# State mixer of a two-block network kernel: chunk-state pairs reordered so that half of them swap array columns, and lag kernels built two chunks at a time

## The chip, the cores and the metric

The kernel runs on one core of a Trainium2 chip. The metric is the device time of one execution in microseconds (us). Before the change the median of three executions is 1320.17 us (1318.69 to 1329.96).

## What is computed

The reference is a chain of layers over 512 tokens of width 1024: a block with a pooling mixer, a gated delta rule and a squared-ReLU feed-forward part, a sparse-attention layer, and then the layer that the change touches, a diagonal state-space mixer (`_s5_mixer`). Everything is float32. That mixer, cut to what matters:

```python
def _s5_mixer(h, w_in, log_dt, lambda_re, lambda_im, b_re, b_im, c_re, c_im, d_skip, w_glu, w_out):
    u, z = jnp.split(h @ w_in, 2, axis=-1)
    u = u.astype(f32).reshape(bsz, seq, G, C)       # 64 groups of 16 channels
    ...
    # per group: 64 complex states, x_t = a x_{t-1} + B u_t,  y_t = Re(C x_t) + D u_t
    ...
    # gelu, gated linear unit, times silu(z), product with w_out
```

Two groups of 64 states are a pair and fill 128 partitions; there are 32 pairs, handled in four quarters (q, or chunk c) of eight pairs p. Time is cut in 64 chunks of 8 frames. Within a chunk the outputs come from a matrix of lags (`Tm`, built from products of powers of B and of C, the lag kernels), and between chunks from states X, which are carried by a scan.

## The kernel before, in words

All large products (weights times activations) run as three float32r products per weight tile, high times high, high times low and low times high (`product`, L403 to L405, helper `half_slot`, L407). Weights come through a ring of four half slots (`RING`): SyncE loads a 128x512 half slot into `raw`, GpSimd (POOL) splits it into `wh` (L1486) and `wl` (L1488) after a tiny instruction (L1485) that waits until TensorE (PE) has used the slot four places back (`half_used`). PE waits for `half_split` before each half slot and uses it in twelve products. So POOL must deliver one half slot in the time of twelve products.

The small float32 products of the state mixer are done in three places.

**Lag kernels** (`lag_kernel`, L713). They are placed in the second half of the feed-forward down product of the first block (`down(1, ...)`, L741): eight output tiles t of four half slots each, and after tiles 1, 2, 3 and 5 one call with c = 0, 1, 2, 3. A call waits for `ca_done` (the powers of C of its chunk, computed by VectorE), and makes 32 products: 8 pairs, real and imaginary part, and two halves. Half 0 reads partitions 0 to 63 and half 1 partitions 64 to 127 (rows of the array); both write PSUM partitions 32c to 32c+31 (columns of the array), in different banks. VectorE (DVE) computes the powers of C in `powers_of_c(c)`, six operations of 128x1152 (L1914 to L1919); for c of 2 and 3 it reuses a buffer, so it first waits for `k_mm`, the count of finished calls:

```python
                if c >= 2:
                    dve.wait_ge(k_mm, c - 1)
                    dve.wait_ge(ca_stored[c % 2], 32)
```

Between two of them DVE adds the finished down tiles (`add_tile`, L1600 and L1601, which frees the PSUM bank, `tile_evicted`) and prepares the next layer's input (`nsa_input`, L1581 and L1591). ScalarE (ACT) stores the powers and, after `k_mm` has reached 4, reads the lag kernels out of PSUM (`store_lags`, L1233).

**Chunk inputs** (`chunk_inputs(q)`, L898, products at L907). 32 products of all 128 rows with 64 columns, 64 long, halves 0 and 1 in turn: each half writes its 64 PSUM partitions.

**Chunk outputs** (`chunk_outputs(q)`, L912). For each p4 of 0 to 3 it makes 12 products of 128 columns' length: four of part 0 (L925, 128 rows, 64 columns, the lag matrix) and eight of parts 1 and 2 (L927, 64 rows, 64 columns, states times powers of C). Of these, half 0 reads partitions 0 to 63 and writes partitions 0 to 63, and half 1 reads and writes 64 to 127. Pair p4 writes PSUM bank 6 and pair p4+4 bank 7.

The two kinds of calls stand between the tiles of the mixer's input product (`in_tile(n)`, two half slots each), in this order: inputs(0), tiles 5 and 6, inputs(1), tile 7, outputs(0), tile 8, turn_outputs(0), inputs(2), tile 9, outputs(1), tile 10, turn_outputs(1), inputs(3), tile 11, outputs(2), tile 12, turn_outputs(2), tile 13, outputs(3), tile 14, turn_outputs(3), tile 15. DVE runs the scan between them (`chunk_states`), ACT's queue issues the regrouping transfers of u (`regroup_u`, L1395), the loads of the lag matrix and of the powers (`load_y`, L1365 and L1366) and reads outputs from PSUM (`evict_y`, L1401), after which `turn_outputs` transposes them (L938).

Of the kernel before, what the change touches and what calls it, by code (L numbers as in the profile page):

```python
# [41 lines left out]
SC = 16  # L42
SP = 64
FR = 8
NC8 = T // FR
NPAIR = SG // 2
# [35 lines left out]
def build(nc, A, scratch, out_dram):  # L82
# [6 lines left out]
    with ctx:  # L89
# [34 lines left out]
        bigB = place("bigB", [128, 16384])  # L124
# [13 lines left out]
        ps = ctx.enter_context(nc.psum_tensor("ps", [128, 8, 512], f32))  # L138
# [97 lines left out]
        uc = view(bigA, 8192, SG, NC8)  # L236
        YH = place("yH", [128, KT, T], f32r, over="bigA", at=48 * KB)
        YL = place("yL", [128, KT, T], f32r, over="uT")
        bq = [view(bigB, 3584 * i, 2, 8, 128) for i in range(2)]
# [19 lines left out]
        CAp = [view(bigB, at, 2, 8, 144) for at in (6400, 12800)]  # L259
# [23 lines left out]
        ca_done = sem("ssm_c_powers")  # L283
# [105 lines left out]
        def _(pe):  # L389
# [141 lines left out]
            for tt in range(TT):  # L531
                pe.wait_ge(l2_std, 5 + tt)
                for h in range(NHG):
                    i = pe.matmul(ps[:, 4 + tt, h * 128:(h + 1) * 128], hd(gB, tt, h), const("cumsum"),
                                  start=True, stop=True)
# [174 lines left out]
                                             baS[c % 2][ri][:, (q * 4 + g) * 128:(q * 4 + g + 1) * 128], ident)  # L710
                        i.then_inc(bt_mm, 1)

            def lag_kernel(c):  # L713

                pe.wait_ge(ca_done, c + 1)
                if c == 0:
                    pe.wait_ge(bt_ev, 16)
                for n in range(8):
                    pair = c * 8 + n
                    for ri in range(2):  # L720
                        for half in range(2):
                            P = slice(64 * half, 64 * half + 64)
                            i = pe.matmul(ps[32 * c:32 * c + 32, 4 + n // 4 * 2 + half, n % 4 * 128:n % 4 * 128 + 128],  # L723
                                          bigB[P, 2048 + 512 * ri + pair * SC:2080 + 512 * ri + pair * SC],
                                          CAp[c % 2][P, ri, n, 0:128], start=ri == 0, stop=ri == 1)
                i.then_inc(k_mm, 1)

            def down(part, after):
                for t in range(8):
                    pe.wait_ge(tile_evicted, TILE0[f"down{part}"] + t - 3)  # L730
                    for h in range(4):
                        half_slot(ps[:, t % 4, :], 2 * SLOT0[f"down{part}"] + 4 * t + h, h,
                                  lambda k: (ffH[:, h * 4 + k, :], ffL[:, h * 4 + k, :]), h == 0, h == 3,
                                  (ff_room, RING_FF + FT // 2 * part + 4 * h) if t == 0 else None)
                    if t in after:
                        after[t]()
# [1 line left out]
            linear("up0", ready=(g_split, KT), between=lambda: sum_squares(1))  # L738
            down(0, {t: lambda c=c: transpose_b(c) for c, t in enumerate((3, 4, 6, 7))})
            linear("up1")  # L740
            down(1, {t: lambda c=c: lag_kernel(c) for c, t in enumerate((1, 2, 3, 5))})  # L741
            linear("nsa", ready=(g_split, 2 * KT), between=lambda: sum_squares(2))

            pe.wait_ge(r_ready, 4)
# [144 lines left out]
            def in_tile(n):  # L889
# [3 lines left out]
                for h in range(2):  # L893
                    half_slot(ps[:, n % (4 if n < 8 else 2), :], 2 * SLOT0["sin"] + 2 * n + h, (2 * n + h) % RING,
                              lambda k: (sH[:, h * 4 + k, :], sL[:, h * 4 + k, :]), h == 0, h == 1,
                              (g_split, 3 * KT + 4 * h) if n == 0 else None)

            def chunk_inputs(q):  # L898

                pe.wait_ge(uc_in[q], 8 * 16)  # L900
                pe.wait_ge(b_in[q % 2], 16 * (q // 2 + 1))
                if q:
                    pe.wait_ge(w_read, q)
                for ri in range(2):
                    for p in range(8):
                        for half in range(2):
                            i = pe.matmul(ps[64 * half:64 * half + 64, 4 + ri, p * 64:p * 64 + 64],  # L907
                                          bq[q % 2][:, ri, p, 64 * half:64 * half + 64], uc[:, q * 16 + half * 8 + p, :],
                                          start=True, stop=True)
                i.then_inc(w_mm, 1)  # L910

            def chunk_outputs(q):  # L912

                pe.wait_ge(t_in, 16 * (q + 1))
                pe.wait_ge(ca_in, 16 * (q + 1))
                pe.wait_ge(x_done, q + 1)
                if q:
                    pe.wait_ge(y_ev, q)
                for p4 in range(4):
                    for part, p in [(0, p4), (0, p4 + 4), (1, p4), (1, p4 + 4), (2, p4), (2, p4 + 4)]:  # L920
                        for half in range(2):
                            P = slice(64 * half, 64 * half + 64)
                            o = ps[P, 6 + p // 4, p % 4 * 128:p % 4 * 128 + 128]
                            if part == 0:
                                i = pe.matmul(o, uc[:, q * 16 + half * 8 + p, :], Tm[:, half, p, :], start=True, stop=False)  # L925
                            else:
                                i = pe.matmul(o, Xq[q % 2][P, part - 1, p, :], CA[P, part - 1, p, :], start=False, stop=part == 2)  # L927
                i.then_inc(y_mm, 1)
# [1374 lines left out]
def lay_out(i):  # L2303
    a = {}
    w_in = i["w_in"][0]
    nsa = i["l0_w_in_2"]
    qcols = np.concatenate([h * DH + np.arange(DH) for h in HEAD_ORDER])
    s = NH * DH
    kv = NG * DH
    zcols = s + 6 * kv + 3 * NH + qcols  # L2310
    branches = [nsa[:, s + b * kv:s + (b + 1) * kv] for b in range(6)]
    nsa_feature = np.concatenate([branches[0], branches[1], nsa[:, qcols], branches[2], branches[4]], 1)
    v_both = np.concatenate([branches[3], branches[5]], 1)
    val = v_both.reshape(4, 2, 128, 512).transpose(0, 2, 1, 3).reshape(4, 128, 1024)
    glu = i["l1_w_glu_2"][SSM_ORDER].reshape(D, 2, KT, 128).transpose(0, 2, 1, 3).reshape(D, 2 * D)
    up = slots(i["w_up"][0])
    down = i["w_down"][0].reshape(4, D, D)
    down = [np.stack([slots(d) for d in down[2 * n:2 * n + 2]], 1).reshape(16, 128, 1024) for n in range(2)]
    stream = np.concatenate([
        slots(w_in[:, :20 * 128]), slots(i["w_out"][0]), up[:16], down[0], up[16:], down[1],  # L2320
        slots(nsa_feature), val, slots(nsa[:, zcols]), slots(i["l0_w_out_2"][qcols]),
        slots(i["l1_w_in_2"][:, np.concatenate([SSM_ORDER, D + np.arange(D)])]), slots(glu), slots(i["l1_w_out_2"])])
    stream = stream.reshape(-1, 128, 2, 512).transpose(0, 2, 1, 3).reshape(-1, 128, 512)
    for name in ("out", "nout", "sout"):
        o = 2 * SLOT0[name]
        stream[o:o + 8] = stream[o + np.array([0, 2, 4, 6, 1, 3, 5, 7])]
    a["wstream"] = stream
    a["x"] = i["x"][0].T.reshape(KT, 128, T).transpose(1, 0, 2)
    a["consts"] = constants()
    a["w_ab"] = tall(w_in[:, 20 * 128:])  # L2330
    a["w_gate"] = tall(nsa[:, s + 6 * kv + np.concatenate([b * NH + np.array(HALF_ORDER) for b in range(3)])])
    a["w_pool"] = i["w_pool"][0].transpose(1, 0, 2).reshape(128, 512)
    for n in "kv":
        a[f"cmp_{n}_w1"] = tall(i[f"l0_cmp_{n}_w1_2"])
        a[f"cmp_{n}_w2"] = tall(i[f"l0_cmp_{n}_w2_2"])

    pair = lambda v: v.reshape(NPAIR, 128, -1).transpose(1, 0, 2).reshape(128, -1)
    a["ssm_b_re"] = pair(i["l1_b_re_2"])
    a["ssm_b_im"] = pair(i["l1_b_im_2"])
    a["ssm_c_re"] = pair(i["l1_c_re_2"].transpose(0, 2, 1))  # L2340
    a["ssm_c_im"] = pair(i["l1_c_im_2"].transpose(0, 2, 1))
    t = dict(norm_mix=by_partition(i["norm_mix"]), norm_mlp=by_partition(i["norm_mlp"]),
             norm_final=by_partition(i["norm_final"]), l0_norm=by_partition(i["l0_norm_2"]),
             l1_norm=by_partition(i["l1_norm_2"]), final_norm=by_partition(i["final_norm_2"]),
             conv=i["conv_w"][0].reshape(CONV, 12, 128).transpose(2, 1, 0).reshape(128, -1),
             pool_scale=by_partition(i["pool_scale"]), gdn_norm=i["gdn_norm"].T,
             a_log=np.broadcast_to(np.tile(i["a_log"][0], TT), (128, 16)),
             dt_bias=np.broadcast_to(np.tile(i["dt_bias"][0], TT), (128, 16)),
             kpe=i["l0_cmp_k_pe_2"].reshape(CMPB // 2, 128).T, vpe=i["l0_cmp_v_pe_2"].reshape(CMPB // 2, 128).T,
             d_skip=by_partition(i["l1_d_2"].reshape(-1)[SSM_ORDER]),  # L2350
             log_dt=np.repeat(i["l1_log_dt_2"].reshape(NPAIR, 2).T, SP, 0),
             lre=pair(i["l1_lambda_re_2"]), lim=pair(i["l1_lambda_im_2"]))
    a["params"] = np.concatenate([t[name] for name in PARAM_W], 1)
    return {n: np.ascontiguousarray(v) for n, v in a.items()}

HEAD_ORDER = [(2 * gp + g2) * 4 + r for gp in range(2) for r in range(4) for g2 in range(2)]

SSM_ORDER = np.concatenate([(2 * (8 * q + p) + half) * SC + np.arange(SC) for q in range(4) for half in range(2) for p in range(8)])  # L2360

# [23 lines left out]
```

## Time and profile before

| what | value |
|---|---|
| median of 3 executions | 1320.17 us (1318.69 to 1329.96) |
| span of the profiled execution (first to last instruction) | 1321.5 us |
| PE busy | 1275.7 us, 97% of the span |
| POOL busy | 856.8 us, 65% |
| DVE busy | 773.1 us, 59% |
| ACT busy | 415.7 us, 31% |

The profiled execution is one more execution of the same program. The page gives its span alone, with no time of its own beside it; the span lies inside the three measured times, 1.3 us above their median. In the profile a float32 product of the small kind stands as two records on PE, so 32 products are x64 rows; a product of float32r (L403 to L405) is one record. PEld is the loading of weights into the array, which runs beside PE. Durations of single products overlap, so the time that a run of products takes is read from the starts.

### The profile page before, as it was taken

How to read it: one execution, taken by the hardware profiler on the slowest of the kernel's cores; microseconds unless marked ns; L12 is line 12 of the kernel's file. 1: busy time of each engine (PE TensorE's matmuls, PEld its weight loads, DVE VectorE, ACT ScalarE, POOL GpSimd, SP SyncE). 2: the span in 40 equal slices, each digit the busy share in tenths (PEclk: the TensorE clock that was granted, in tenths of full speed). 3: DMA queues.
4: the chain of work that ended last, by engine and by line, in shares of the span. 5: the costliest groups of instructions: out<-in, count | busy, mean ns of one | idle time of the engine just before them, and what ended most of it. 6: DMA issues, size and time to landing. Idle time of an engine off the chain costs nothing.

```text
span 1321.5 us, 21957 instructions
## 1 busy us (share of the span) xinstructions
PE 1275.7 (97%) x7698; PEld 1002.5 (76%) x7698; DVE 773.1 (59%) x1101; ACT 415.7 (31%) x851; POOL 856.8 (65%) x1078
## 2 busy tenths in 40 slices
PE   7999999999998999999999999899999999999996
PEld 5778897878876888888788798455557787878884
DVE  6968665589699011597447235268774559832223
ACT  4175745343201133212200021477772300331111
POOL 7767631978999777899678718212215875467872
PEclk9999999999999999999999999889999999999998
DMA  5222100342325432344394213100005359623231
GB/s 204 90 64 80 49 4 8 107 138 95 96 79 199 160 96 98 108 145 152 103 351 131 78 33 91 37 1 1 1 1 195 124 144 269 209 71 98 95 96 72
DMA packets 86620, 137.89 MB, mean 104 GB/s; under 512 B 16528, under 2 KB 34448, under 8 KB 85520
## 3 DMA queue, kind: packets, MB, share of 16 engines
q1 hardware_dynamic: 48384, 88.10, 21.4%
q10 hardware_dynamic: 38160, 48.71, 11.7%
q8 instruction: 55, 0.90, 0.3%
q14 instruction: 21, 0.17, 0.0%
HBM read 119.02 MB, written 20.91 MB: 106 GB/s over the span
## 4 chain that ended last, share of the span: by engine, by line
PE 80%; DVE 8%; issue 4%; POOL 3%; ACT 2%; DMA 1%; ACTq 1%; POOLq 0%; DVEq 0%
PE ps L403 20%; PE ps L404 19%; PE ps L405 19%; PE ps L839 3%; PE ps L819 3%; PE ps L863 3%; PE ps L573 2%; POOL small L1485 2%; PE ps L723 1%; PE ps L768 1%; PE ps L927 1%; POOL wh L1486 1%; PE ps L563 1%; DVE bigB L1632 1%; DVE bigA L2096 1%
## 5 line engine op out<-in xcount | busy, mean ns | idle before, releaser
L1488 POOL TENSOR_TENSOR wl<-raw,wh 128x512 fp32r<-128x512 f32 x336 | 496.6, 1478 | 26.9
L1485 POOL TENSOR_TENSOR small<-small 1x1 f32<-1x1 f32 x336 | 125.2, 373 | 258.1 <-PE ps L405 217.5
L403 PE MATMUL ps<-uH,wh 128*128 128x512 f32 x664 | 262.8, 396 | 1.5 <-DVE uL L1581 1.5
L404 PE MATMUL ps<-uL,wh 128*128 128x512 f32 x664 | 259.2, 390 | 0.0
L405 PE MATMUL ps<-uH,wl 128*128 128x512 f32 x664 | 259.2, 390 | 0.0
L1486 POOL CAST wh<-raw 128x512 fp32r<-128x512 f32 x336 | 203.4, 605 | 0.0
L403 PEld LDWEIGHTS ps<-uH,wh 128*128 128x128 f32 x664 | 125.2, 189 | 29.6 <-DVE uL L1581 1.9
L404 PEld LDWEIGHTS ps<-uL,wh 128*128 128x128 f32 x664 | 125.2, 189 | 27.4 <-issue 1.7
L405 PEld LDWEIGHTS ps<-uH,wl 128*128 128x128 f32 x664 | 125.1, 188 | 26.1
L403 PE MATMUL ps<-ffH,wh 128*128 128x512 f32 x256 | 101.4, 396 | 4.3 <-POOL wl L1488 4.3
L1553 POOL TENSOR_TENSOR bigA<-small 128x512 f32<-128x512 f32 x16 | 16.7, 1041 | 128.6 <-PE ps L872 100.0
L404 PE MATMUL ps<-ffL,wh 128*128 128x512 f32 x256 | 99.9, 390 | 0.0
L405 PE MATMUL ps<-ffH,wl 128*128 128x512 f32 x256 | 99.7, 390 | 0.0
L2078 DVE CUSTOM_DVE_ANT_0 bigB<-ps,bigB 128x512 f32<-128x512 f32 (+3 forms) x128 | 57.4, 486 | 40.3 <-issue 25.1
L1350 ACT ACTIVATE bigB<-bigB,small 128x512 f32<-128x512 f32 (+3 forms) x128 | 70.3, 551 | 31.8 <-DVE small L2078 31.8
L1601 DVE TENSOR_TENSOR hT<-hT,ps 128x512 f32<-128x512 f32 x40 | 27.4, 686 | 67.1 <-PE ps L405 66.6
L403 PEld LDWEIGHTS ps<-ffH,wh 128*128 128x128 f32 x256 | 48.0, 188 | 18.1 <-POOL wl L1488 6.1
L839 PEld LDWEIGHTS ps<-const_table,bigB 128*128 128x128 f32 x320 | 34.7, 143 | 32.8 <-issue 21.9
L1930 DVE TENSOR_TENSOR ffL<-bigB,ffH 128x512 f32 x16 | 11.1, 692 | 79.9 <-ACT ffH L1268 79.9
L405 PEld LDWEIGHTS ps<-ffH,wl 128*128 128x128 f32 x256 | 48.1, 188 | 10.3
L819 PE MATMUL ps<-bigA 64*128 64x512 f32 (+3 forms) x256 | 54.8, 508 | 1.1 <-ACT bigB L1331 0.7
L404 PEld LDWEIGHTS ps<-ffL,wh 128*128 128x128 f32 x256 | 48.1, 188 | 9.4
(405 smaller groups left out, 2409.2 us busy)
## 6 DMA issues: line engine op xcount, KB each, us to landing
raw<-wstream SPq DMA_DIRECT2D x336, 256.0 KB, 2.6
b_powers_scratch<-bigB ACTq DMA_DIRECT2D x4, 1024.0 KB, 4.9
c_powers_scratch<-bigB ACTq DMA_DIRECT2D x8, 512.0 KB, 4.2
lags_scratch<-lag_rows_scratch ACTq DMA_DIRECT2D x8, 512.0 KB, 8.4
bigB<-b_powers_scratch ACTq DMA_DIRECT2D x4, 1024.0 KB, 9.6
bigB<-lags_scratch ACTq DMA_DIRECT2D x4, 1024.0 KB, 6.7
bigB<-c_powers_scratch ACTq DMA_DIRECT2D x4, 1024.0 KB, 10.1
hT<-x ACTq DMA_DIRECT2D x4, 512.0 KB, 7.2
```

What stands on the lines that cost most here:

```text
L403: pe.matmul(out, lh, rh, start=first, stop=False)
L404: pe.matmul(out, lh, rl, start=False, stop=False)
L405: return pe.matmul(out, ll, rh, start=False, stop=last)
L819: i = pe.matmul(ps[:, u % 2 * 2 + half, 0:W], nsT[P, t, qt * 128:(qt + 1) * 128], nsT[P, 12 + 2 * b + t // 4, 0:W], start=True, stop=True)
L839: i = pe.transpose(ps[:, 4 + at // 512, at % 512:at % 512 + 128], prob[:, u % 6, half, kt * 128:(kt + 1) * 128], ident)
L863: i = pe.matmul(ps[64 * half:64 * half + 64, 7, kt * 128:512], vtok[:, kt, b * 256 + h * DH:b * 256 + (h + 1) * DH], probT[g % 2][:, half, ...
L1350: i = act.activation(prob[:, n % 6, half, 0:W], prob[:, n % 6, half, 0:W], ACT.Exp, scale=-1.0, bias=anmax[:, n % 3, half:half + 1], accum ...
L1485: pool.tensor_tensor(small[0:1, 569 + j:570 + j], zero_ap[0:1], zero_ap[0:1], ALU.add)
L1486: pool.tensor_copy(wh[:, j, :], raw[:, j, :]).then_inc(half_lead, 1)
L1488: pool.tensor_tensor(wl[:, j, :], raw[:, j, :], wh[:, j, :].bitcast(f32), ALU.subtract).then_inc(half_split, 1)
L1601: dve.tensor_tensor(hT[:, n, :], hT[:, n, :], ps[:, n % 4, :], ALU.add).then_inc(tile_evicted, 1)
L2078: i = dve.tensor_tensor_reduce(prob[:, u % 6, half, 0:W], ps[:, u % 2 * 2 + half, 0:W], dsl[t % 2][:, half, 512 - W:512], -1.0, 3e38, ALU. ...
```

## The change

Pairs are put in another order of groups (`PAIR_ORDER`): for pairs with p of 4 to 7 in each quarter the two groups change places, so that partitions 0 to 63 hold the second group (half 1) and partitions 64 to 127 the first. In `chunk_outputs` the products of these pairs still read their rows, but write the columns of their half: rows 0 to 63 go to PSUM partitions 64 to 127, and the reverse. The four products of the pairs p4 and p4+4 in one part thus use four different quarters (64 rows by 64 columns) of the array. `chunk_inputs` takes u of the half that belongs to the rows and is otherwise the same. The lag kernels are made by `lag_kernels(c)` for the chunks c and c+1 together, 64 products: for each pair and part, two chunks (different columns) times two row halves. It is called after down tiles 2 and 5 (c = 0 and 2) and waits for the powers of both its chunks; it adds 2 to `k_mm`.

```diff
-            def lag_kernel(c):
-                pe.wait_ge(ca_done, c + 1)
+            def lag_kernels(c):
+                pe.wait_ge(ca_done, c + 2)
                 if c == 0:
                     pe.wait_ge(bt_ev, 16)
                 for n in range(8):
-                    pair = c * 8 + n
                     for ri in range(2):
-                        for half in range(2):
-                            P = slice(64 * half, 64 * half + 64)
-                            i = pe.matmul(ps[32 * c:32 * c + 32, 4 + n // 4 * 2 + half, n % 4 * 128:n % 4 * 128 + 128],
-                                          bigB[P, 2048 + 512 * ri + pair * SC:2080 + 512 * ri + pair * SC],
-                                          CAp[c % 2][P, ri, n, 0:128], start=ri == 0, stop=ri == 1)
-                i.then_inc(k_mm, 1)
+                        for at in (c, c + 1):
+                            pair = at * 8 + n
+                            for rows in range(2):
+                                P = slice(64 * rows, 64 * rows + 64)
+                                half = rows if n < 4 else 1 - rows
+                                i = pe.matmul(ps[32 * at:32 * at + 32, 4 + n // 4 * 2 + half, n % 4 * 128:n % 4 * 128 + 128],
+                                              bigB[P, 2048 + 512 * ri + pair * SC:2080 + 512 * ri + pair * SC],
+                                              CAp[at % 2][P, ri, n, 0:128], start=ri == 0, stop=ri == 1)
+                i.then_inc(k_mm, 2)
...
-            down(1, {t: lambda c=c: lag_kernel(c) for c, t in enumerate((1, 2, 3, 5))})
+            down(1, {t: lambda c=c: lag_kernels(c) for c, t in ((0, 2), (2, 5))})
...
+            def half_of(p, rows):
+                return rows if p < 4 else 1 - rows
...
-                        for half in range(2):
-                            i = pe.matmul(ps[64 * half:64 * half + 64, 4 + ri, p * 64:p * 64 + 64],
-                                          bq[q % 2][:, ri, p, 64 * half:64 * half + 64], uc[:, q * 16 + half * 8 + p, :],
+                        for rows in range(2):
+                            half = half_of(p, rows)
+                            i = pe.matmul(ps[64 * rows:64 * rows + 64, 4 + ri, p * 64:p * 64 + 64],
+                                          bq[q % 2][:, ri, p, 64 * rows:64 * rows + 64], uc[:, q * 16 + half * 8 + p, :],
                                           start=True, stop=True)
...
-                        for half in range(2):
-                            P = slice(64 * half, 64 * half + 64)
-                            o = ps[P, 6 + p // 4, p % 4 * 128:p % 4 * 128 + 128]
+                        for rows in range(2):
+                            half = half_of(p, rows)
+                            P = slice(64 * rows, 64 * rows + 64)
+                            o = ps[64 * half:64 * half + 64, 6 + p // 4, p % 4 * 128:p % 4 * 128 + 128]
...
-    pair = lambda v: v.reshape(NPAIR, 128, -1).transpose(1, 0, 2).reshape(128, -1)
+    pair = lambda v: v[PAIR_ORDER].reshape(NPAIR, 128, -1).transpose(1, 0, 2).reshape(128, -1)
...
-             log_dt=np.repeat(i["l1_log_dt_2"].reshape(NPAIR, 2).T, SP, 0),
+             log_dt=pair(np.repeat(i["l1_log_dt_2"][:, None], SP, 1)),
...
+PAIR_ORDER = [2 * n + (half if n % 8 < 4 else 1 - half) for n in range(NPAIR) for half in range(2)]
```

How the lag kernels move on PE is seen after down tiles 1 and 2. Before, the first call, which waits for the stored powers of B and for the powers of C, stands between tiles 1 and 2:

```order
1868 L405 MATMUL ps<-ffH,wl 128x512
1869 L723 MATMUL ps<-bigB 32x128 [waits ssm_b_stored,ssm_c_powers]
1870 L723 MATMUL ps<-bigB 32x128 x31
1871 L403 MATMUL ps<-ffH,wh 128x512 [waits half_split,tile_evicted]
1872 L404 MATMUL ps<-ffL,wh 128x512
1873 L405 MATMUL ps<-ffH,wl 128x512
1874 L403 MATMUL ps<-ffH,wh 128x512
```

In the changed kernel tile 2 follows tile 1 at once, and the first call, now of 64 products (L725), stands 48 products (four half slots) later, behind tile 2:

```order
1916 L405 MATMUL ps<-ffH,wl 128x512
1917 L725 MATMUL ps<-bigB 32x128 [waits ssm_b_stored,ssm_c_powers]
1918 L725 MATMUL ps<-bigB 32x128 x63
1919 L403 MATMUL ps<-ffH,wh 128x512 [waits half_split,tile_evicted]
1920 L404 MATMUL ps<-ffL,wh 128x512
1921 L405 MATMUL ps<-ffH,wl 128x512
```

DVE's instructions are the same in both kernels. This is where its third chunk of powers begins, behind the addition of down tile 1:

```order
335 L1600 TENSOR_TENSOR ps<-ps,rms 128x512 [waits half_used,tile_evicted,ssm_c_powers]
336 L1601 TENSOR_TENSOR hT<-hT,ps 128x512 [waits dve_chain]
337 L1581 SCALAR_TENSOR_TENSOR uL<-hT,small,uH 128x512 [waits weighted_lead]
338 L1914 TENSOR_TENSOR bigB<-bigB 128x1152 [waits ssm_c_powers_even_stored,lag_kernel_product]
339 L1915 TENSOR_TENSOR bigB<-bigB 128x1152 [waits dve_chain]
```

Its wait for `lag_kernel_product` (`k_mm`) was for a call behind tile 1 and is now for one behind tile 2.

## Rows read from the trace of the kernel before

**Rows 1.** The page: busy time per engine, and TensorE's granted clock in 40 slices

```profile
PE 1275.7 (97%) x7698; PEld 1002.5 (76%) x7698; DVE 773.1 (59%) x1101; ACT 415.7 (31%) x851; POOL 856.8 (65%) x1078
...
PEclk9999999999999999999999999889999999999998
```

**Rows 2.** PE timeline, first lag call: start, length, line, operation, records

```profile
562.37 0.39 PE L404 MATMUL ps<-ffL,wh 128*128 128x512 f32 x1
562.60 0.39 PE L405 MATMUL ps<-ffH,wl 128*128 128x512 f32 x1
562.92 3.68 PE L723 MATMUL ps<-bigB 64*32 64x128 f32 x64
566.53 0.50 PE L403 MATMUL ps<-ffH,wh 128*128 128x512 f32 x1
566.87 0.40 PE L404 MATMUL ps<-ffL,wh 128*128 128x512 f32 x1
```

**Rows 3.** PE timeline, chunk outputs(0) to chunk inputs(2)

```profile
1095.21 0.66 PE L925 MATMUL ps<-bigB,bigA 128*64 128x128 f32 x8
1095.80 1.09 PE L927 MATMUL ps<-bigB 64*64 64x128 f32 x16
1096.82 0.66 PE L925 MATMUL ps<-bigB,bigA 128*64 128x128 f32 x8
...
1101.64 0.50 PE L403 MATMUL ps<-sH,wh 128*128 128x512 f32 x1
...
1108.36 1.09 PE L938 MATMUL ps<-const_table,bigB 128*128 128x128 f32 x8 [0.96 <-ACT bigB L1401]
1110.68 2.08 PE L907 MATMUL ps<-bigA,bigB 128*64 128x64 f32 x64 [1.24 <-DMA bigA<-u_scratch]
1112.70 0.50 PE L403 MATMUL ps<-sH,wh 128*128 128x512 f32 x1
```

**Rows 4.** The chain in order of time: a product that fills the whole array

```profile
765.00 14.29 PE ps L768 x128
```

**Rows 5.** POOL timeline, the half slots of down tile 2 being split

```profile
560.62 2.29 POOL L1488 TENSOR_TENSOR wl<-raw,wh 128x512 fp32r<-128x512 f32 x1
...
564.79 2.27 POOL L1488 TENSOR_TENSOR wl<-raw,wh 128x512 fp32r<-128x512 f32 x1
...
568.95 2.29 POOL L1488 TENSOR_TENSOR wl<-raw,wh 128x512 fp32r<-128x512 f32 x1
...
572.01 1.62 POOL L1488 TENSOR_TENSOR wl<-raw,wh 128x512 fp32r<-128x512 f32 x1
```

**Rows 6.** Busy time by stretch: without powers of C, with them, after them

```profile
505.00:520.00 15.00, 15.00 (x68) 12.40 (x67) 2.08 (x3) 4.51 (x8) 10.98 (x18) 1.00 0.25 88
...
560.00:575.00 15.00, 15.00 (x115) 12.55 (x114) 14.76 (x10) 1.96 (x4) 14.68 (x13) 1.00 0.55 160
...
620.00:635.00 15.00, 15.00 (x92) 12.49 (x87) 5.54 (x6) 4.15 (x8) 12.45 (x17) 1.00 0.57 150
```

**Rows 7.** DVE timeline, powers of C of chunk 2, end of chunk 3, and tile 5

```profile
572.41 2.44 DVE L1914 TENSOR_TENSOR bigB<-bigB 128x1152 f32<-128x1152 f32 x1
...
583.22 1.77 DVE L1919 TENSOR_TENSOR bigB<-bigB 128x1152 f32<-128x1152 f32 x1
...
600.95 1.78 DVE L1919 TENSOR_TENSOR bigB<-bigB 128x1152 f32<-128x1152 f32 x1
...
618.18 0.70 DVE L1600 TENSOR_TENSOR ps<-ps,rms 128x512 f32<-128x512 f32 x1 [2.74 <-PE ps L405]
```

**Rows 8.** ACT timeline: transfers issued and outputs read between the chunk products

```profile
1097.47 8.70 ACTq L1395 DMA_DIRECT2D bigA<-u_scratch  x8
1106.21 0.46 ACTq L1365 DMA_DIRECT2D bigB<-lags_scratch  x1
...
1107.28 1.02 ACT L1401 ACTIVATE bigB<-ps 128x1024 f32<-128x1024 f32 x1 [51.93 <-issue]
...
1126.77 1.02 ACT L1401 ACTIVATE bigB<-ps 128x1024 f32<-128x1024 f32 x1
```

## The prediction

> **What bounds the kernel now.** I read the page first: PE is busy in 1275.7 us of the span, 97%, and no other engine passes 65% [rows 1]. The granted clock is 9 tenths or more in nearly every slice, so the 2.4 GHz level holds in the stages that matter here. The kernel is PE's program, and a product saved there is time saved, unless PE then waits for something that had been just in time. So I read PE's timeline around the changed products, and after that POOL, DVE and ACT in the same stretches, to see what is just in time.
>
> A step of the large products is 0.23 us (562.37 to 562.60) [rows 2], a half slot of twelve 2.72 us, a down tile 10.9 us. A lag call takes PE from the start of the last L405 (562.60) to the next L403 (566.53), less one step: 3.70 us, and the next step is 0.34 in place of 0.23, so 3.8 us in all. The 32 products in it take 3.61 us, 113 ns each [rows 2]. A product of the whole array and nearly the same length takes 14.29/64 = 223 ns [rows 4]. So two row halves of the array already work at the same time, and each product costs half its own length. The same in chunk outputs: eight L927 take 1.02 us (1095.80 to 1096.82) and four L925 take 0.59 us (1095.21 to 1095.80), four times each, together 6.43 us up to 1101.64 [rows 3]. Eight at 113 ns are 0.90 us, so some 0.12 us of each block is the switch between shapes. Chunk inputs take 2.02 us for 32 products 64 long, 63 ns each [rows 3]: there the two column halves overlap.
>
> **Part 1, the products by four.** Nothing in the trace has four quarters of the array at work. What it shows is that two row halves overlap and that two column halves overlap, each nearly fully. The price of a product that shares the array with three others lies between 113 ns (only two at a time, as now) and 56 ns (half of it). PE can start products at least every 63 ns, as chunk inputs show, with their weight loads [rows 3]; whether it can start them at 56 is open. I take 60, near the row of 63, since that row is itself bound by two products of 64 columns' length (half of 113 is 56, so it has only 6 to 7 ns of its own above it).
>
> The Trainium skill (TensorE: Matmul & The Clock Gate, section "Wait — 56ns, not 53.3ns?") says that with the firmware decoding instructions the sequencer spends about 62 ns per MATMUL. A float32 product is two records, so by this rule it would cost 124 ns and four quarters could bring nothing. The row of 63 ns per product of two records [rows 3] goes against it: 31 ns per record.
>
> Lag kernels: 64 products at 60 are 3.84 us; with the 0.2 us at the edges (3.8 less 3.6) a call is 4.0 us. Before four calls of 3.8 = 15.2, after two of 4.0 = 8.0: 7.2 us less of PE's work. Bounds: two calls of 3.8, saving 7.6; or two of 7.4, saving 0.4.
>
> Chunk outputs: a block of eight L927 becomes 0.48 + 0.12 = 0.60 us in place of 1.02, so 0.42 less, 1.7 us a call. Bounds: 0.45 a block, 1.8 a call, and nothing. The L925 use full rows; their columns now come 0, 1, 1, 0 in place of 0, 1, 0, 1, still two different ones in each couple: no change. Chunk inputs: the same products on the same rows and columns; only which u they read differs. The reordered tables are prepared before the launch: nothing.
>
> **Part 2, what covers the saving in the down product.** POOL in the same stretch is the point. Without powers of C it is busy 11.0 of 15 us and waits for PE; with them it is busy 14.7 of 15 and gets through 13 instructions in place of 18 (three a half slot), while DVE is busy 14.8 of 15 [rows 6]. One L1488 lasts up to 2.29 us there, 1.62 in a gap of DVE. Four half slots of tile 2 are ready at 562.9, 567.1, 571.2 and 573.6 (start plus length) [rows 5]. So POOL delivers one in 4.2 us while the powers run, and PE uses one in 2.72. Now the lag call gives PE 3.8 us to do elsewhere, and PE never waits. With the call gone from behind tile 1, PE would use the first at 562.9 to 565.6, wait 1.5 us for the second, use it until 569.8, wait 1.4 for the third, use it until 573.9 and end tile 2 at 576.7. So 2.9 us of the 3.8 are given back at once.
>
> DVE then: its third chunk of powers started at 572.41 [rows 7] and waits now for the call behind tile 2, which ends at 576.7 + 4.0 = 580.7. DVE stands 8 us; in this time POOL runs undisturbed and fills the ring, so tiles 3 and 4 run through. Behind the waiting instruction are the addition of tile 2, the next chunk of powers and all later additions. PE needs the addition of tile 2 for its tile 6, over 30 us later: no wait. The powers of chunk 2 took 572.4 to 585.0 and those of chunk 3 ended at 602.7. Moved by 8 us, the last end at about 610. The second call, behind tile 5, needs them at about 615, so this wait costs nothing, by a margin of some 5 us. But the slow stretch of POOL now lies over tile 5, and takes from PE what it took in tile 2: I estimate 1.3 us, half as much, as POOL enters it with a full ring. After it DVE had 2.7 us of idle time before tile 5's addition [rows 7] and is busy 5.5 of 15 us after 620 [rows 6]; it catches up before tile 7 ends. So the down product gives 7.2 - 2.9 - 1.3 = 3.0 us.
>
> **Part 3, what covers the saving in the input product.** Behind chunk outputs(0) PE already waits twice: 0.96 us for ACT's reading of the outputs and 1.24 for the regrouped u [rows 3]. The reading at 1107.28 stands behind ten issues in ACT's queue, 1097.47 to about 1107 [rows 8], which do not wait for these products. So inputs(2) starts at 1110.68 whatever outputs(0) takes, and its 1.7 us are lost. The other three are not covered: PE goes without a wait from 1112.70 on, POOL is ahead, and the next reading (1126.77 + 1.02 = 1127.8, held by ACT's own work ahead of it) is done before PE would want it at about 1128.7 [rows 8]. The loads of the lag matrix are issued when outputs end and so move with them. So 3 x 1.7 = 5.1 us.
>
> **Sum.** 3.0 + 5.1 = 8.1 us. From the profiled span of 1321.5 that is 1313.4; from the median of the runs, 1.3 us below it, 1312.1. I say 1312.
>
> **Rivals.**
>
> *Only two at a time.* If the array or its instruction queue does not take four, products stay at 113 ns. For it: no row shows four. Against: both kinds of couples overlap nearly fully. Then outputs save nothing, two lag calls of 7.4 us save 0.4, but tile 2 still loses 2.9 to POOL, and tile 5 about 1: slower by 3.5 us, 1323.6. The kernel gets slower from the point where a lag call of 64 products takes over 5.5 us (83 ns each: 15.2 - 2 x 5.5 = 4.2 is what POOL takes back), if the outputs stay as they are. Chance 0.2.
>
> *Partial overlap.* Products at 75 to 95 ns, from weight loads or starts that don't fit. Lags break even, outputs give a third to a half: 1317 (about 3 x 1 us). Chance 0.15.
>
> *Banks.* The array takes four in the lag kernels, where each row half writes a bank of its own, but not in the outputs, where both row halves write bank 6 and then both bank 7. Then only the lags' 3.0 count: 1317. Against: the L927 of now already write one bank from both row halves and overlap all the same [rows 3]. The Trainium skill has it as a rule (TensorEngine Tiling (Array Packing), "Gotcha 1: PSUM Pressure"): different row tiles cannot access the same bank at the same time. The trace disagrees with it for different partitions of a bank, by 1.02 us for eight. Chance 0.05.
>
> *POOL takes nothing*, because PE's earlier pace moves DVE and POOL too: 7.6 + 5.4 = 13.0 less, 1307. Against: the ready times of POOL [rows 5] are set by DVE's powers, which do not depend on PE there. Chance 0.05.
>
> **How the numbers follow.** The forecast has 0.55. Two at a time 0.2, partial 0.15, banks 0.05, POOL free 0.05. A measurement of this kernel tells about 1% from no change, 13 us. Only the last rival comes near it, so faster by over 1% has 0.04; slower by over 1% would need a stall that I have not found, 0.03; within 1% 0.93. The range reaches from just under the last rival, 1307, to just above two at a time, 1324.5. The runs before spread up to 1330, which the range does not take in.
>
> **What would show it.** Right: x128 records of the new lag call in about 3.9 us, twice; blocks of the states' products of about 0.60 us; PE waiting for POOL's L1488 in down tiles 2 and 5, some 3 and 1 us; DVE idle for about 8 us before the third powers; wait for u before inputs(2) grown by 1.7 us; PE's end of down tile 7 some 3 us earlier, and 5 us more gained at tile 15. Wrong: blocks still of 1.02 us; a PE wait for DVE before the second lag call; or no PE wait for POOL at all.

## The result and the profile after

The changed kernel takes 1316.39 us, the median of 11 runs (1312.10 to 1318.76), beside 1321.38 us before on the same chips (11 runs, 1318.69 to 1329.96). The ratio is 0.9948 with a 95% interval of 0.9930 to 0.9967: 6.9 us less (4.4 to 9.2). The medians alone lie 5.0 us apart, which is inside this interval. Forecast were 8.1 us less. The change is clear of noise, and smaller than 1%.

The profiled execution ran 1316.44 us with a span of 1314.6. Its page, to be laid beside [rows 1]; the columns are the same:

```profile
PE 1264.4 (96%) x7698; PEld 989.5 (75%) x7698; DVE 776.1 (59%) x1101; ACT 415.5 (32%) x851; POOL 856.5 (65%) x1078
...
L403 PE MATMUL ps<-ffH,wh 128*128 128x512 f32 x256 | 101.8, 398 | 7.9 <-POOL wl L1496 7.7
```

The second line has PE's idle time before the first product of a weight tile, over both halves of the down product: 7.9 us. Before it was 4.3, all of it in the first half. What was added lies in the second half, `down(1, ...)`, where the lag kernels are, as the waits below show. The first lag call and what stands around it, in PE's timeline (start, length, operation, records), answers to [rows 2]:

```profile
576.60 0.39 PE L404 MATMUL ps<-ffL,wh 128*128 128x512 f32 x1
576.82 0.39 PE L405 MATMUL ps<-ffH,wl 128*128 128x512 f32 x1
577.14 3.70 PE L725 MATMUL ps<-bigB 64*32 64x128 f32 x128
580.77 0.50 PE L403 MATMUL ps<-ffH,wh 128*128 128x512 f32 x1
```

64 products now take 3.63 us (577.14 to 580.77), 57 ns each, as long as 32 did before. Four work at a time, at practically the whole of the possible gain. The same in the chunk outputs, beside [rows 3]:

```profile
1092.88 0.66 PE L933 MATMUL ps<-bigB,bigA 128*64 128x128 f32 x8
1093.46 0.67 PE L935 MATMUL ps<-bigB 64*64 64x128 f32 x16
1094.06 0.66 PE L933 MATMUL ps<-bigB,bigA 128*64 128x128 f32 x8
...
1106.00 1.28 PE L946 MATMUL ps<-const_table,bigB 128*128 128x128 f32 x8 [2.63 <-ACT bigB L1409]
1107.90 3.10 PE L914 MATMUL ps<-bigA,bigB 128*64 128x64 f32 x64 [0.63 <-DMA bigA<-u_scratch]
1110.94 0.50 PE L403 MATMUL ps<-sH,wh 128*128 128x512 f32 x1
```

A block of eight products of states takes 0.60 us (1093.46 to 1094.06) in place of 1.02. Two things are seen behind the outputs: the wait for ACT has grown from 0.96 to 2.63 us, and chunk inputs(2) take 3.04 us (1107.90 to 1110.94) in place of 2.02.

The waits in the second half of the down product (who waited, for whom, total, times, longest) show where the rest of the gain went. Before there was no wait of PE for POOL there at all.

```profile
DVE bigB L1922 <- PE ps L725: 8.3, 1, 8.3
PEld ps L403 <- POOL wl L1496: 5.4, 5, 1.5
PE ps L403 <- POOL wl L1496: 3.4, 4, 1.1
```

The two lines for PE speak of the same waits. A large product is drawn 0.39 us long while the next starts after 0.23, so the row of PE hides a part of each wait; the row of the weight loads, 5.4 us, is nearer to what was lost.

To see where the whole kernel gains, I cut each profile in stages by starts on PE: the **down stage**, from the last of the B-power transposes (L709 before) to the last L405 of down tile 7, and the **mixer stage**, from the first product of input tile 0 to turn_outputs(3).

| stage, us | before | after | difference |
|---|---|---|---|
| down stage | 189.5 | 187.0 | -2.5 |
| between the two | 401.97 | 401.93 | 0.0 |
| mixer stage | 124.2 | 119.7 | -4.5 |
| rest to the end | 151.95 | 151.94 | 0.0 |

The stages gain 7.1 us together; the spans differ by 6.9, since the changed kernel reaches the down stage 0.2 us later. The two stages with changed code hold all of the gain. This is one profile of each kernel, and the mixer stage does not come out alike in all executions: more of that under the clock, below.

### The profile page after: what moved, and what is told of

It reads as the page before. It is cut to its first block, busy times and chain, and to the rows that moved or that the text cites. A ratio compares the mean times of both kernels' runs of the same rounds, so it can differ in the third digit from the quotient of the medians.

```text
span 1314.6 us, 21957 instructions
## 1 busy us (share of the span) xinstructions
PE 1264.4 (96%) x7698; PEld 989.5 (75%) x7698; DVE 776.1 (59%) x1101; ACT 415.5 (32%) x851; POOL 856.5 (65%) x1078
## 4 chain that ended last, share of the span: by engine, by line
PE 75%; DVE 8%; issue 6%; POOL 6%; ACT 3%; DMA 1%; ACTq 1%; POOLq 0%; DVEq 0%
PE ps L403 18%; PE ps L405 18%; PE ps L404 18%; PE ps L841 4%; PE ps L821 3%; POOL small L1493 3%; PE ps L865 3%; PE ps L573 2%; POOL wh L1494 2%; POOL wl L1496 1%; PE ps L770 1%; PE ps L563 1%; DVE bigB L1640 1%; DVE bigA L2104 1%; DVE bigA L1666 1%
## 5 line engine op out<-in xcount | busy, mean ns | idle before, releaser
L405 PE MATMUL ps<-uH,wl 128*128 128x512 f32 x664 | 259.1, 390 | 0.0
L405 PEld LDWEIGHTS ps<-uH,wl 128*128 128x128 f32 x664 | 125.0, 188 | 25.9
L405 PE MATMUL ps<-ffH,wl 128*128 128x512 f32 x256 | 99.7, 390 | 0.0
L405 PEld LDWEIGHTS ps<-ffH,wl 128*128 128x128 f32 x256 | 48.1, 188 | 10.2
L1599 DVE TENSOR_TENSOR acc<-acc,xs 128x512 f32<-128x512 f32 x41 | 55.1, 1356 | 0.7
```

The lines of the kernel that those rows point to most:

```text
L405: return pe.matmul(out, ll, rh, start=False, stop=last)
L1599: dve.tensor_tensor(acc[:, i, :], acc[:, i, :], xs[:, i if n == 2 else k % 2, :], ALU.add).then_inc(sq_added, 1)
```

## The experiments

**Each part alone.** First the outputs with the old placing of lag calls, one chunk each:

```diff
-                pe.wait_ge(ca_done, c + 2)
+                pe.wait_ge(ca_done, c + 1)
...
-                        for at in (c, c + 1):
+                        for at in (c,):
...
-            down(1, {t: lambda c=c: lag_kernels(c) for c, t in ((0, 2), (2, 5))})
+            down(1, {t: lambda c=c: lag_kernels(c) for c, t in enumerate((1, 2, 3, 5))})
```

> The reordered pairs with the lag kernels made one chunk at a time behind down tiles 1, 2, 3 and 5, as before. My account: the saving of the changed kernel is the sum of separate parts, and this one is the outputs. The eight products of a block take 0.60 us in place of 1.02 as in the changed kernel; outputs(0) is covered by the wait behind tile 8, the other three save 1.7 us each, the lower clock behind the wait costs 1.0 us less what the wait gives back: about 4.5 us less than before (0.3%), and no PE wait for POOL in the down product. Rival (the two parts help each other, since the lag kernels reach the mixer through the same loads): less than 3 us.

Measured: ratio 0.9964 (0.9939 to 0.9990), 4.8 us less (the medians lie 2.3 us apart). The down stage is 189.5 us, as before, with no wait for POOL; the mixer stage 121.1, that is 3.1 less, where 4.5 were expected.

Then the lag kernels two at a time, pairs and outputs as before:

```diff
-            down(1, {t: lambda c=c: lag_kernel(c) for c, t in enumerate((1, 2, 3, 5))})
+            down(1, {t: lambda c=c: lag_kernels(c) for c, t in ((0, 2), (2, 5))})
```

> The lag kernels two chunks at a time behind down tiles 2 and 5, the chunk outputs as before. My account: PE's work falls by 7.6 us, and POOL's splitting of weights takes back 2 to 3 us in tile 2 and 2 to 3 us in tile 5, so the end of down tile 7 comes 2.5 us earlier and the whole kernel is 2.5 us faster (0.2%). If POOL's part is only a coincidence of one profile: up to 7 us faster.

Measured: ratio 0.9969 (0.9942 to 0.9995), 4.1 us less (the medians lie 3.4 us apart), an interval that takes in 2.5. The down stage is 187.05 us, 2.5 less, with the same waits for POOL as the changed kernel (PE row 3.4, weight loads 5.5) and DVE's wait of 8.3. The mixer stage is 125.5, which is 1.2 more than before, for a reason that comes below. The parts do not quite add up in the stages: 2.5 and 3.1 are 5.6, and less the 1.2 they are 4.4, beside 7.0 for the change. All of this difference is in the mixer stage.

**Who takes back the saving of the lag kernels.** The changed kernel with chunks 0 and 1 in calls of their own behind tiles 1 and 2, so that DVE needn't wait, and only the last two chunks together:

```diff
-            down(1, {t: lambda c=c: lag_kernels(c) for c, t in ((0, 2), (2, 5))})
+            down(1, {t: lambda c=c, n=n: lag_kernels(c, n) for c, n, t in ((0, 1, 1), (1, 1, 2), (2, 2, 5))})
```

> As the changed kernel, but chunk 0 alone behind tile 1 and chunk 1 alone behind tile 2 (32 products each), and chunks 2 and 3 together behind tile 5. PE has 3.8 us more work than in the changed kernel, DVE does not wait 8 us before its third powers. My theory (POOL's splitting is the bound of tiles 2 to 5 while DVE computes powers, so a lag call there is free): tile 1 to 3 as before, the call taken from behind tile 3 is lost in waits for POOL in tiles 4 and 5, the end of tile 7 comes at most 0.5 to 1 us earlier than before, and the kernel is 1.5 to 2 us slower than the changed one. Rival (PE's own work is what counts, and DVE's 8 us wait is what costs): DVE's wait gone, tile 7 ends 3.8 us earlier than before, and the kernel is faster than the changed one by 1 us.

PE's timeline, the waits and the last call:

```profile
596.12 0.50 PE L403 MATMUL ps<-ffH,wh 128*128 128x512 f32 x1 [0.39 <-POOL wl L1496]
600.26 0.50 PE L403 MATMUL ps<-ffH,wh 128*128 128x512 f32 x1 [1.13 <-POOL wl L1496]
604.41 0.50 PE L403 MATMUL ps<-ffH,wh 128*128 128x512 f32 x1 [1.14 <-POOL wl L1496]
618.33 3.70 PE L725 MATMUL ps<-bigB 64*32 64x128 f32 x128
```

PE has a call of 3.8 us less than before, and the last call starts at 618.33, where it started at 618.08 before. The three waits lie 4.15 us apart, which is POOL's pace while the powers run. The down stage is 189.3 us, 0.2 less than before: a whole lag call taken out, and all but 0.2 us of it lost. DVE has no wait for a lag call here, so its wait was not what cost. In time this version and the changed one are not told apart (0.9953, 0.9932 to 0.9975); the 2.3 us between their down stages are shown by the profiles.

The other test takes POOL's burden away. In both kernels four of the six operations of each chunk's powers are left out, which leaves the state mixer with other numbers. Each was run once; what is read is the down stage:

```diff
-                own(dve.tensor_tensor(tv[0], pp[0], cc[0], ALU.mult))
-                own(dve.tensor_tensor(tv[1], pp[1], cc[1], ALU.mult))
-                own(dve.tensor_tensor(o[0], tv[0], tv[1], ALU.add))
-                own(dve.tensor_tensor(tv[0], pp[0], cc[1], ALU.mult))
-                own(dve.tensor_tensor(tv[1], pp[1], cc[0], ALU.mult))
-                dve.tensor_tensor(o[1], tv[0], tv[1], ALU.subtract).then_inc(ca_done, 1)
+                own(dve.tensor_tensor(o[0], pp[0], cc[0], ALU.mult))
+                dve.tensor_tensor(o[1], pp[1], cc[1], ALU.mult).then_inc(ca_done, 1)
```

> The kernel before with four of the six operations of each chunk's powers of C left out (o[0] and o[1] are one product each; the state mixer computes other numbers). Nothing on PE changes. With DVE's powers short, POOL should keep its ring full. PE had no wait in tiles 2 to 5 before, so the end of down tile 7 stays at about 643.7 us (offset of the start aside).

> The changed kernel with the same four operations of each chunk's powers left out. My theory (POOL, slowed by DVE's powers, takes back 5 of the 7.6 us that PE saves): PE's waits for POOL in tiles 2 and 5 are gone, and tile 7 ends 7 to 7.6 us earlier than in the kernel before with the same cut. Rival (what is lost comes from the later call itself, DVE's wait for it or the cost of the call): it still ends only 2.5 to 4 us earlier.

Waits of the changed kernel with the cut, from 540 to 645 us:

```profile
DVE bigB L1922 <- PE ps L725: 11.8, 1, 11.8
...
PE ps L403 <- DVE uL L1589: 1.5, 1, 1.5
```

The second line belongs to the next layer (640.7 us; the down stage ends at 634.0). No wait for POOL is left; DVE's wait for the call is longer than ever, 11.8 us, and costs nothing. The down stage is 189.5 us in the kernel before with the cut, just as without it, and 181.8 in the changed one with it: 7.7 us less, where the two calls of 3.8 us that went are 7.6. So 5.2 of 7.7 us are what POOL takes back in the changed kernel while DVE computes the powers; with the powers cut short, nothing is taken back.

**Filling the wait behind outputs(0).** The wait for ACT and then for u in the mixer stage is as long as something else lets it be. In the first try input tile 9 goes ahead of both:

```diff
             in_tile(8)
+            in_tile(9)
             turn_outputs(0)
             chunk_inputs(2)
-            in_tile(9)
             chunk_outputs(1)
```

> As the changed kernel, but input tile 9 moved ahead of turn_outputs(0) and chunk inputs(2), so that PE has 5.5 us of products in the place where it waits 2.6 us for ACT and 0.6 us for u, and outputs(1) follow inputs(2) at once. My theory: both waits vanish, the granted clock stays at its higher level there, inputs(2) takes 2.0 us in place of 3.0, so 4.2 us less than the changed kernel; outputs(1) needs no wait, as its states were ready long before. Rival (the transfer of u and the states' scan come later and are then waited for elsewhere): chunk outputs(2) waits for DVE, since its scan starts 2 to 3 us later, and the gain is under 2 us.

```profile
1108.58 1.03 PE L946 MATMUL ps<-const_table,bigB 128*128 128x128 f32 x8
1109.54 2.08 PE L914 MATMUL ps<-bigA,bigB 128*64 128x64 f32 x64
1115.64 0.66 PE L933 MATMUL ps<-bigB,bigA 128*64 128x128 f32 x8 [4.01 <-issue]
```

Both waits are gone and inputs(2) are back at 2.0 us, but outputs(1) wait 4.0 us. Neither I nor the rival had this place. The releaser isn't named ("issue"), but the trace has it: the load of the powers of their quarter was issued at 1104.10 and took 11.4 us to land, which is 1115.5, and outputs(1) start at 1115.64. The clock falls there too, behind the wait: it is at half from 1116.7 to 1120.1, and a block of states takes 1.06 us in it (1117.98 to 1119.04). The mixer stage is 120.3 us, no gain on 119.7. The whole kernel has 0.9930 of the time before (0.9901 to 0.9958), which is not told apart from the changed one. The second try leaves tile 10 ahead of outputs(1):

```diff
             in_tile(8)
+            in_tile(9)
             turn_outputs(0)
             chunk_inputs(2)
-            in_tile(9)
-            chunk_outputs(1)
             in_tile(10)
+            chunk_outputs(1)
+            in_tile(11)
             turn_outputs(1)
             chunk_inputs(3)
-            in_tile(11)
             chunk_outputs(2)
...
             regroup_u(3)
+            evict_z(9)
             act.wait_ge(x_done, 2)
             load_e(3)
             gelu(0)
-            evict_z(9)
```

> As the changed kernel, with another order of the input tiles: outputs(0), tiles 8 and 9, turn_outputs(0), inputs(2), tile 10, outputs(1), tile 11, turn_outputs(1), inputs(3), outputs(2), tile 12 and on as before; ACT reads tile 9 ahead of the load of rotations. The first try put outputs(1) ahead of tile 10, and PE waited 4.0 us for the lag matrix and powers of quarter 1 there. My theory: those loads are the limit of this stretch (they are issued when the previous outputs end and share the DMA engines with the regrouping of u), so with tile 10 ahead of outputs(1) the wait goes, outputs(2) waits 2 us at most, and turn_outputs(3) comes 3 to 4 us earlier than in the changed kernel. Rival (the loads only move the wait on to outputs(2) and (3)): PE waits 3 to 4 us there instead, and nothing is gained.

```profile
1104.73 2.09 PE L914 MATMUL ps<-bigA,bigB 128*64 128x64 f32 x64
...
1123.74 2.08 PE L914 MATMUL ps<-bigA,bigB 128*64 128x64 f32 x64
1127.72 0.66 PE L933 MATMUL ps<-bigB,bigA 128*64 128x128 f32 x8 [1.90 <-issue]
```

One wait of 1.9 us is left, again until the load of powers lands (issued at 1118.9, 8.7 us to landing, so 1127.6), and the mixer stage is 116.7 us: 3.0 less than the changed kernel. The kernel has 0.9930 of the time before (0.9908 to 0.9952), the same as the first try, whose stage was no shorter. Whether it is faster than the changed kernel I then tried on one chip:

> The changed kernel once more, on the same chip as the reordered version. By the stages of the profiles (down product 2.5 us shorter, input product of the mixer 4.5 us shorter) 7.0 us less than before, a ratio of 0.9947. If the lower clock behind outputs(0) is a regular part of the change, its profile shows it again at that place, with inputs(2) at 3.0 to 3.6 us in place of 2.0.

> The reordered version once more. By its stages (2.5 us in the down product, 7.6 in the input product) 10.1 us less than before, a ratio of 0.9924, and so 3 us faster than the changed kernel on the same chip. The profile shows inputs(2) at 2.0 us, the clock at its higher level throughout the stretch, and the wait of 1.9 us before outputs(2). Rival (its first runs were fast by chance of the start and of other stages): no more than 1 us apart from the changed kernel.

Measured: 0.9954 (0.9939 to 0.9969) for the changed kernel, 0.9945 (0.9920 to 0.9970) for the reordered one, both with a median of 1314.02 us. The stages repeat to 0.3 us, 119.9 and 116.4 in the mixer. The whole does not tell them apart: the reordered kernel's runs go from 1310.2 to 1324.8. So it is shown that the stage is 3 us shorter, and not shown that the kernel is faster.

**How the array takes the products.** Another order of the eight products within a block:

```diff
-                    for part, p in [(0, p4), (0, p4 + 4), (1, p4), (1, p4 + 4), (2, p4), (2, p4 + 4)]:
+                    for part, p in [(0, p4), (0, p4 + 4), (1, p4), (2, p4), (1, p4 + 4), (2, p4 + 4)]:
```

> As the changed kernel, but within a block the eight products of states go in the order part 1 of pair p4, part 2 of pair p4, part 1 of pair p4+4, part 2 of pair p4+4, so that only two quarters differ among neighbours and each quarter comes twice before the others. Theory A (products are taken in order, and one whose quarter is busy holds back all behind it): the first four and the last four take as in the kernel before, save where the second and third couple meet, a block takes about 0.8 to 1.0 us. Theory B (each quarter has its own short queue, and products pass each other): 0.60 us, as in the changed kernel.

Measured: a block of states takes 0.61 us (1093.81 to 1094.42), as in the changed kernel. Four products of two quarters stand ahead of four of the other two. Taken strictly in order, a block would need 0.8 us or more by my estimate, so theory A falls. The starts say the same: four records start within 0.05 us (1093.80 to 1093.85), where the kernel before, with two quarters, has two within 0.11. So at this distance the products of free quarters are not held back by those ahead of them. The kernel was run once.

Eight tiles of 64 rows by 32 columns, in the second lag call:

```diff
-                        for at in (c, c + 1):
+                        for at in (c, c + 1) if c == 0 else range(4):
```

> As the changed kernel, but the second lag call makes products for all four chunks in turn (128 of them, in eight tiles of 64 rows by 32 columns); the products of chunks 0 and 1 are made again there from the powers of chunks 2 and 3, so these lag kernels hold other numbers. If the array takes as many tiles as there are (starts of two records lie 7 ns apart, eight fit in the 109 ns of a step): 128 products in 3.6 to 3.9 us. If four is the limit of what runs at a time: 7.2 us. If starts with their weight loads are the limit at some 25 ns a record: 6.4 us.

```profile
615.88 2.26 PE L725 MATMUL ps<-bigB 64*32 64x128 f32 x145
619.21 1.80 PE L725 MATMUL ps<-bigB 64*32 64x128 f32 x111 [1.08 <-issue]
620.94 0.50 PE L403 MATMUL ps<-ffH,wh 128*128 128x512 f32 x1
```

128 products take 5.06 us, and 1.35 of these are one gap between two starts, 617.86 to 619.21. Without it they take 3.7 us, 29 ns each, and each of the two stretches runs at about this pace (145 records in 1.98 us, 111 in 1.73): inside them, eight work at a time as four do. The profile doesn't say what the gap waits for ("issue"), and no run settles it; with it a product costs 40 ns. This kernel, too, was run once.

## Why the prediction was right, point by point

- **Products by four**: I took 60 ns from a range of 56 to 113; it is 57, for the reason that I gave, four parts of the array at work. The rivals of two at a time (113 ns), partial overlap and banks are out, and so is the one in which POOL takes nothing. PE's saving in the down product is 7.6 us, not 7.2.
- **Tile 2 and POOL**: 2.9 us were to be given back. From the last L405 of tile 1 to that of tile 2 pass 14.04 us (562.78 to 576.82), where 48 steps need 10.9: 3.2.
- **Tile 5 and POOL**: I estimated 1.3 us, half of tile 2's. From 580.77, tiles 3 to 5 need 143 steps of 0.227 and the slow one's 0.11, up to 613.3; the last L405 starts at 615.44: 2.1. This term was sized too small. I had POOL enter the slow stretch with a full ring, but DVE's third powers had already slowed it: its subtractions start 4.2 us apart at 585.27 and 589.45, and again at 598.98, 603.14 and 607.32 beside the fourth. Two chunks of powers, one behind the other, use the ring up.
- **DVE**: its third powers wait 8.3 us (8 forecast), the fourth end at 610.8 (610), the second call starts at 615.76 (615) without a wait. The cut kernel, which loses nothing beside a wait of 11.8 us, shows that such a wait is free.
- **Down product in all**: 2.5 us beside 3.0. The saving was 0.4 larger than forecast, and tiles 2 and 5 took 0.3 and 0.8 more; 0.2 of the measured 2.5 is in none of these readings.
- **Outputs**: 0.60 us a block, as said, 1.70 us a call (1116.60 to 1121.34 beside 6.44). The wait for ACT behind outputs(0) swallows the first: it grows by 1.67 us. The other three are gained, 5.1 us. The start of inputs(2) did move a little, against what I wrote: counted from the start of the stage, it comes 0.4 us earlier (64.9 in place of 65.3).
- **The load for outputs(1)**: I wrote that the loads move with the outputs. For this one that was a misreading: in [rows 8] it stands behind the eight transfers of u, and it is issued 60.8 us after the start of the stage in both kernels. Its powers landed at 1118.1, 0.3 us before outputs(1) started at 1118.40; in the changed kernel they land at 1115.4, 1.2 us before 1116.60. So it cost nothing, but outputs(1) could not start more than 1.2 us earlier, which is what the first try of filling the wait ran into.
- **What I missed**: the clock. I had read it for the kernel before, where it stays up in this stretch, and carried that over. In the changed kernel it falls to half, the 1.2 GHz level, from 1106.8 to 1110.2. The first line is of the kernel before, the others of the changed one:

```profile
1107.00:1110.60 3.60, 1.49 (x10) 0.86 (x8) 2.96 (x4) 1.51 (x2) 2.77 (x4) 1.00 1.21 200
1103.00:1106.80 3.80, 1.17 (x9) 0.80 (x8) 3.73 (x3) 1.51 (x2) 3.22 (x4) 1.00 1.32 204
1106.80:1110.20 3.40, 2.77 (x46) 2.38 (x46) 2.90 (x4) 0.00 (x0) 0.00 (x0) 0.50 0.99 369
```

(stretch, its length, busy time of PE, PEld, DVE, ACT and POOL, granted clock, DMA share, GB/s.) In the 3.8 us ahead of the fall, from the last product of tile 8 on, PE is busy 1.17; before the change it was 1.49 of 3.6 in the same place, and the clock stayed. Chunk inputs(2) fall right into the slow stretch and take 1.0 us more. So the mixer stage gives 5.1 for the three outputs, 0.4 for the earlier start of inputs(2), and loses 1.0 by the clock: the measured 4.5.

This term is not the same in every execution. In this place the clock fell in all seven profiles that have the short outputs(0) and the old order of tiles, for 3.4 us in the two of the changed kernel and for 6.8 us in the other five. Of the three profiles with the long outputs(0) it fell in one, the lag kernels alone, for 3.4 us, and inputs(2) took 3.3 us; that is most of the 1.2 us which that kernel lost there. In the five with a fall of 6.8 us the mixer stage takes 121.1 to 122.8 us (in the longest, PE's wait for ACT is 4.2 us as well), a gain of 3.1 to 1.4 on the kernel before and not of 4.5. With the wait filled (second try) the clock stayed up in both profiles. That the longer idle time of PE brings the fall is what these profiles suggest, and no run shows it alone.

So 2.5 + 4.5 = 7.0 stands beside 3.0 + 5.1 = 8.1. The mechanisms in the down product and in the outputs were right. Two terms of the sum were well off, tile 5 by 0.8 and the clock, put at nothing, by 1.0; tile 2 was off by 0.3. The larger saving of the lag calls and the earlier inputs(2) made up for 0.8 of these. That the sum came so near is in part luck: with the mixer stage as in those five profiles it would have been 3.9 to 5.6.

## What to carry to other kernels

Small products gain from using different parts of the array at a time. With two and four parts they did so at nearly the full factor here. But read first who was just keeping up while PE did them. A pause of PE for small products is time in which a producer catches up, and if that producer runs at its limit in the stretch (its busy share and pace show it), the saved pause comes back as a wait. And a wait of PE that gets longer can cost twice, as the clock may fall behind it. Other products put into the wait made the stage 3 us shorter here, though the whole time did not show it; and a load that nobody waited for can be the next limit, so look up when it lands.

## What the runs showed of the hardware that I had not expected

- Two, four and eight tiles of float32 products run at the same time at nearly the full rate: 113, 57 and 29 ns a product of 128 columns' length, beside 223 with the whole array. The last figure is from one run and leaves a gap of 1.35 us out; with it, it is 40.
- Products of two free quarters are not held back by four products ahead of them (0.61 us a block in the other order, 0.60 in the first).
- DVE's operations on 128x1152 slow POOL's splitting to about 4.2 us a half slot (the three waits shown with chunks 0 and 1 apart lie 4.15 apart), where its subtractions in the changed kernel start 2.05 us apart with DVE idle (574.56, 576.62, 578.66); and DVE's operations too can be shorter when POOL is idle: the second of the third chunk starts at 583.24, where POOL does nothing until 583.9, and takes 1.36 us where 1.78 is the usual least.
- The clock at the same instructions differs between executions. The second profile of the reordered kernel has the lower level for 13.7 us in the attention layer, with PE busy throughout. Ahead of it PE was busy 9.8 of 10.4 us, with one wait of 0.51. The stretch between the two stages takes 408.2 us there, beside 397.3 to 402.0 in the others:

```profile
653.00:782.00 129.00, 128.37 (x665) 107.35 (x663) 50.03 (x65) 11.90 (x17) 85.21 (x116) 1.00 0.49 154
782.50:796.00 13.50, 13.50 (x53) 12.44 (x53) 9.12 (x14) 5.03 (x6) 0.00 (x0) 0.50 0.00 1
```

Such differences outside the changed code are as large as the change itself, which is why I go by the stages more than by the total; and the mixer stage, as said, varies too.
